# Hybrid encoder layer with expert-choice MoE on one core: attention preparation reordered, matmuls added during the first gather, two split rows instead of three on GpSimd, last result in halves

## The reference, cut to what matters

```python
proj = einsum('bsd,de->bse', rmsnorm(x), w_in)            # q, k, v, xr, gate
q, k = axial_rope(rmsnorm(q)), axial_rope(rmsnorm(k))
attn = softmax(q @ k.T * scale) @ v
lru  = (rglru_forward(conv(xr)) + rglru_backward(conv(xr))) * gelu(gate)
x    = x + concat(attn, lru) @ w_out
h    = rmsnorm(x)
affinity = softmax(h @ router_w)                          # (tokens, 16)
gate_vals, tok_idx = top_k(affinity.T, 64)                # per expert and group
xs  = take(h, tok_idx)
hid = silu(xs @ w_gate[e]) * (xs @ w_up[e])
ys  = (hid @ w_down[e]) * gate_vals
y   = x + zeros.at[tok_idx].add(ys)
```

## Time and profile before

| | us |
|---|---|
| median of 3 runs | 1058.98 (1057.98 to 1059.56) |
| profiled execution, time | 1058.12 |
| its span in the trace | 1056.2 |
| PE busy | 984.7 (93%) |
| DVE busy | 818.7 (78%) |
| ACT busy | 747.0 (71%) |
| POOL busy | 338.2 (32%) |
| share of PE in the chain that ended last | 82% |

### The profile page before, as it was taken

One profiled execution on the slowest core, in us unless ns is written; L12 is line 12 of the kernel. 1 busy time (PEld: TensorE's weight loads), 2 busy tenths in 40 slices (PEclk: granted clock), 3 DMA queues, 4 the chain that ended last, 5 costly groups with the idle time before them and its releaser, 6 DMA issues.

```text
span 1056.2 us, 15145 instructions
## 1 busy us (share of the span) xinstructions
PE 984.7 (93%) x5035; PEld 826.2 (78%) x5035; DVE 818.7 (78%) x1079; ACT 747.0 (71%) x1002; POOL 338.2 (32%) x175
## 2 busy tenths in 40 slices
PE   5999999977999999928999999999999999999994
PEld 4997998856777788827888888888888888888883
DVE  5749898787787224784989888988898889988983
ACT  6447888467797455545878877887788777877772
POOL 1000000132396111141056435643464346513320
PEclk9999999989999999968999999999999999999998
DMA  8110111000301633368999999999999999999842
GB/s 283 36 46 6 46 40 41 1 0 7 115 1 63 239 120 120 120 242 342 409 392 410 388 384 392 405 386 385 391 400 383 383 393 400 382 384 372 323 163 36
DMA packets 75265, 248.97 MB, mean 236 GB/s; under 512 B 9380, under 2 KB 16600, under 8 KB 75224
## 3 DMA queue, kind: packets, MB, share of 16 engines
q1 hardware_dynamic: 70616, 231.65, 57.1%
q0 software_dynamic: 4608, 16.78, 6.2%
HBM read 231.63 MB, written 16.78 MB: 235 GB/s over the span
## 4 chain that ended last, share of the span: by engine, by line
PE 82%; DVE 7%; ACT 5%; issue 3%; POOL 1%; DMA 1%; ACTq 0%; SPq 0%; POOLq 0%; DVEq 0%
PE bank L972 25%; PE bank L974 24%; PE bank L973 24%; PE bank L978 6%; DVE e_lo L1619 2%; ACT e_hi L899 2%; PE bank L1149 1%; PE bank L1107 1%; PE bank L1108 1%; PE bank L1007 1%; DMA x_nat<-in_x_prompt_dram 1%; ACT prob L843 1%; DMA xs<-h_rows,idx_all 0%; POOL prob L619 0%; DVE row_stat L1453 0%
## 5 line engine op out<-in xcount | busy, mean ns | idle before, releaser
L972 PE MATMUL bank<-e_hi,xsT_hi 128*128 128x512 f32 x512 | 202.4, 395 | 0.7 <-DVE xsT_lo L1624 0.6
L974 PE MATMUL bank<-e_hi,xsT_lo 128*128 128x512 f32 x512 | 200.5, 392 | 0.0
L973 PE MATMUL bank<-e_lo,xsT_hi 128*128 128x512 f32 x512 | 200.1, 391 | 0.0
L651 POOL COPY idx_now<-idx_all 128x1 uint32 (+1 forms) x16 | 157.1, 9818 | 27.2 <-DMA y_dram<-ys,idx_now 27.2
L899 ACT ACTIVATE e_hi<-raw_gate 128x1024 fp32r<-128x1024 f32 x128 | 134.7, 1062 | 35.3 <-PE bank L974 33.7
L1619 DVE TENSOR_TENSOR e_lo<-raw_down,e_hi 128x1024 fp32r<-128x1024 f32 x128 | 146.9, 1219 | 2.4 <-ACT e_hi L899 0.2
L1619 DVE TENSOR_TENSOR e_lo<-raw_gate,e_hi 128x1024 fp32r<-128x1024 f32 x125 | 144.7, 1219 | 4.8 <-ACT e_hi L899 4.7
L1619 DVE TENSOR_TENSOR e_lo<-raw_up,e_hi 128x1024 fp32r<-128x1024 f32 x128 | 146.7, 1219 | 1.4 <-ACT e_hi L899 1.3
L899 ACT ACTIVATE e_hi<-raw_up 128x1024 fp32r<-128x1024 f32 x128 | 126.5, 1057 | 1.3 <-PE bank L974 0.3
L899 ACT ACTIVATE e_hi<-raw_down 128x1024 fp32r<-128x1024 f32 x128 | 125.0, 1058 | 0.4 <-PE bank L974 0.3
L972 PEld LDWEIGHTS bank<-e_hi,xsT_hi 128*128 128x128 f32 x512 | 96.8, 189 | 21.4 <-DVE e_lo L1619 1.0
(11 more groups left out here) (241 smaller groups left out, 2193.9 us busy)
## 6 DMA issues: line engine op xcount, KB each, us to landing
raw_gate<-in_exp_w_gate_dram SPq DMA_DIRECT2D x64, 1024.0 KB, 10.8
raw_up<-in_exp_w_up_dram SPq DMA_DIRECT2D x64, 1024.0 KB, 8.2
raw_down<-in_exp_w_down_dram SPq DMA_DIRECT2D x64, 1024.0 KB, 7.0
w_raw<-in_w_in_dram SPq DMA_DIRECT2D x6, 1024.0 KB, 5.4
wo_raw<-in_w_out_dram SPq DMA_DIRECT2D x8, 512.0 KB, 4.2
y_dram<-x SPq DMA_DIRECT2D x8, 512.0 KB, 5.1
h_rows<-h SPq DMA_DIRECT2D x8, 512.0 KB, 2.6
x_nat<-in_x_prompt_dram SPq DMA_DIRECT2D x4, 512.0 KB, 7.5
```

The source lines that it names most:

```text
L651: pool.tensor_copy(idx_now[:, 2:3], idx_all[:, bass.ds(e, 1)] if not isinstance(e, int) else idx_all[:, e:e + 1]).then_inc(idx_copied, 1)
L972: pe.matmul(out, l_hi, r_hi, start=first, stop=False)
L973: pe.matmul(out, l_hi, r_lo, start=False, stop=False)
L974: return pe.matmul(out, l_lo, r_hi, start=False, stop=last)
```

## The change

Seven edits, in four places.

1. **Values.** `v_hi` and `v_lo` become one tensor for each group of tokens. The first group's split, and rotation and scaling of unit 9, move from slots 2 to 4 to `LRU_AT[27]`, which stands before the copy of job 27; the second group's split goes to slot 16. POOL zeroes each group's tensors apart.
2. **Places beside the slots.** The splits of blocks 4 to 7 move to slots 3/4, 8/9, 13/14 and 19/20. Transposes n from 12 on stand at 6, 8, 10, ... 28, and each copy in the slot of its transpose.
3. **Pairs 1 and 2.** Their first value matmuls are left out of their slot and done in the next, with that slot's own.
4. **During the first gather.** PE runs 16 matmuls 128x512 on `e_hi` row 0, whose results nothing reads, between the turned indices and the gathered tokens.
5. **Rows.** POOL writes the low parts of two rows of the first expert, DVE of the third too.
6. **Search.** In the last block, `find(1, 0)` stands behind the copy of `x2T`, and `find(1, 1)` behind `rstd2`.
7. **The end.** The last product runs rows 0 and 1 for both halves, then rows 2 to 7 for half 0, then for half 1. ACT scales each half by itself, and POOL scatters each half (128 rows of 512), with indices 2i and 2i+1 that DVE computes once behind `routed`.

```diff
-    v_hi = at("v_hi", R1 + 80 * K, [P, NB, VW], F32R)
-    v_lo = at("v_lo", R1 + 90 * K, [P, NB, VW], F32R)
+    v_hi = [at(f"v_hi{s}", R1 + o * K, [P, BPS, VW], F32R) for s, o in enumerate((80, 90))]
+    v_lo = [at(f"v_lo{s}", R1 + o * K, [P, BPS, VW], F32R) for s, o in enumerate((97, 85))]
...
-    SPLIT, POOL_ROWS = 6, 3
+    SPLIT, POOL_ROWS, WARM = 6, 2, 16
...
+    lru_at(27, ("v", 0), ("rotate", UNITS_QK - 1), ("norm", UNITS_QK - 1))
...
-    beside = {2: [('v', 0)], 3: [('rotate', 9)], 4: [('norm', 9)], 6: [('hi', 4)], 7: [('lo', 4)], 10: [('hi', 5)], 11: [('lo', 5)], 15: [('hi', 6)], 16: [('lo', 6)], 22: [('hi', 7)], 23: [('lo', 7)]}
+    beside = {3: [("hi", 4)], 4: [("lo", 4)], 8: [("hi", 5)], 9: [("lo", 5)], 13: [("hi", 6)], 14: [("lo", 6)],
+              16: [("v", 1)], 19: [("hi", 7)], 20: [("lo", 7)]}
     for n in range(2 * BPS, USES * NB):
-        at_slot = n - 2 * BPS + 1 if n < EARLY else 10 + (n - EARLY) * 5 // 3
+        at_slot = n - 2 * BPS + 1 if n < EARLY else 6 + (n - EARLY) * 2
         beside.setdefault(at_slot, []).append(("transpose", n))
-        beside.setdefault(at_slot + 1, []).append(("out", n))
+        beside.setdefault(at_slot, []).append(("out", n))
...
+    def late_pair(v):
+
+        return v % (2 * BPS) == 0 and 0 < v // (2 * BPS) < PAIRS_ONE_BANK
+
+    def pv_at(u):
+
+        v = u - V_LAG
+        if not 0 <= v < UNITS or late_pair(v):
+            return []
+        return [v - 1, v] if late_pair(v - 1) else [v]
...
-        for e in range(E - 4, E):
+        for e in range(E - 4, E - 1):
             scatter_step(e, 2 * (E - 4) + e - (E - 4) + 1)
+        y_halves = y.rearrange("t (h c) -> (t h) c", h=2)
+        pool.wait_ge(routed, 3)
+        for h in range(2):
+            pool.wait_ge(ys_done, E + 1 + h)
+            pool.sem_inc(scatter_ready, 1)
+            pool.indirect_dma_start(y_halves, bass.IndirectOffsetOnAxis(ap=idx_half[:, h:h + 1], axis=0),
+                                    ys[:, h * D // 2:(h + 1) * D // 2], None, compute_op=ALU.add).then_inc(scattered, 16)
+        pool.wait_ge(scattered, 16 * (E + 1))
...
-        act.wait_ge(row_used, 24 * E + 8)
-        results(E - 1)
+        act.wait_ge(ys_free, E)
+        for h in range(2):
+            act.wait_ge(row_used, 24 * E + 8 - SPLIT + h + 1)
+            act.activation(ys[:, h * D // 2:(h + 1) * D // 2], bank[:, 4 + h, :], ACT.Copy, scale=gate_all[:, E - 1:E]).then_inc(ys_done, 1)
...
+        pe.wait_ge(row_hi, 1)
+        for n in range(WARM):
+            pe.matmul(bank[:, n % 2, :], e_hi[:, 0, 0:P], e_hi[:, 0, 0:512], start=True, stop=True)
         pe.wait_ge(routed, 2)
         turn_tokens(16, 0)
...
-        rows(24 * E, 0, 4, hidT_hi, hidT_lo, {})
+        for j in range(8 - SPLIT):
+            pe.wait_ge(row_lo, 24 * E + j + 1)
+            for h in range(2):
+                ins = last_product(j, h)
+            ins.then_inc(row_used, 1)
+        for h in range(2):
+            for j in range(8 - SPLIT, 8):
+                if h == 0:
+                    pe.wait_ge(row_lo, 24 * E + j + 1)
+                ins = last_product(j, h)
+            ins.then_inc(row_used, 1)
...
-                find(1, 0)
                 dve.wait_ge(x2T_done, 2 * b + 1)
                 dve.wait_ge(logits_done, b - 1)
                 dve.tensor_copy(x2T[:, b % 2, 0:4, :], bank[:, 4, :].rearrange("p (k t) -> p k t", k=4)).then_inc(x2T_out_v, 1)
-                find(1, 1)
+                find(1, 0)
...
+        dve.wait_ge(routed, 1)
+        for h in range(2):
+            ins = dve.tensor_scalar(half_row[:, h:h + 1], idx_all[:, E - 1:E], 2.0, float(h), ALU.mult, ALU.add)
+        link(ins)
+        dve.tensor_copy(idx_half[:, :], half_row).then_inc(routed, 1)
```

63 lines of the change are left out of this document (41 added, 22 removed).

## The result

| | before | after |
|---|---|---|
| median (runs) | 1058.59 (4) | 1039.32 (1039.12 to 1039.55, 4) |
| span of the profiled execution | 1056.2 | 1037.0 |
| PE busy | 984.7 (93%) | 984.8 (95%) |

The ratio is 0.9817, 95% interval 0.980 to 0.9834: 19.3 us less. The forecast was 1038.2 (1033.5 to 1046.0). The spans differ by 19.2, and PE is busy as long as before: what went is waiting (span less busy time fell from 71.5 to 52.2). The 16 added matmuls do not show in PE's busy time, which fits a shorter time at half clock.

What follows compares the result with a forecast made beforehand. PE was taken as busy throughout the expert loop, so only its waits and half clock before or behind it count. Terms summed to 20.8 us off a median of 1058.98, giving 1038.2 us (range 1033.5 to 1046.0).

Steps and rivals of the forecast that it cites:

- attention's start: Values' split, rotation and scaling moved into DVE's 4.70 us hole: slot 9 starts 6.6 us sooner (4.5 to 7.5).
- bank 7: Slots 10 to 28: PE's four waits before transposes into bank 7 all go, 5.4 us (lower bound 2.7).
- pairs: Output bank at the change of pairs: two waits of 3.3 us shrink to 1.3, winning 2.0 us (0 to 3.3).
- half clock in attention: Half clock behind the 1.9 us wait at the change of pairs goes too: 1.6 us (0 to 1.6).
- two rows on GpSimd: Before the first expert: GpSimd ends its rows before DVE's merge, which takes 0.15; 1.6 us won (1.3 to 1.7).
- 16 matmuls: During the first gather: token transposes and first 36 expert matmuls run at full clock; 2.9 us won (0 to 3.9).
- the end: Last product, scaling and scatter in halves: PE held 0.7, scaling -0.5, scatter -0.9; sum -0.7 us (-1.8 to +0.8).
- the walk: Step-by-step timing of attention's slots: transposed probabilities may start at 215.1, first value product ends at 219.9, pair's product reached at 235.05.
- Rival 1: DVE sets attention's pace, with only 7% to spare: gain 14.0 us, time 1045.0; chance 0.21.
- Rival 4: Slower: attention's copies act as a lockstep, holding the next maximum and exponential while PE waits; 1068.6 us, chance 0.04.
- third rival: First gather held behind DVE's four rows, all behind it 3.8 us later: 1042.0, or 1044.9 without clock gain; chance 0.06.
- Rival 2: Clock does not rise in time: 16 matmuls all at half, 2.9 and 0.6 us lost, 1041.7; chance 0.07.

Runs made afterwards that it cites:

- m1_mix: Changed kernel with the copies of pairs 0 and 1 out of their bank one slot earlier on ACT and DVE; median 1039.40 us, ratio 0.9815.
- a2_places: Changed kernel with the late value matmuls of pairs 1 and 2 put back in their own slot; median 1041.55 us, ratio 0.9846.
- r3_rows: Changed kernel with three low rows on GpSimd again, not two; median 1040.66 us, ratio 0.9830.
- w0_no_warm: Changed kernel without the 16 matmuls ahead of the gathered tokens; median 1041.33 us, ratio 0.9838.
- f0_find: Changed kernel with the index search ahead of the x2T copy again; median 1039.46 us, ratio 0.9815.
- t0_tail: Changed kernel with the end of before: both halves in each row, one scaling, one scatter; median 1039.75 us, ratio 0.9815.
- g1_issue: Changed kernel with DVE's low rows made to wait for the first gather's issue, and 14 matmuls, not 16; median 1040.45 us, ratio 0.9827.

## Why the prediction held, and where it did not

| step | forecast | in the trace of after |
|---|---|---|
| attention's start | 6.6 | 5.6 |
| bank 7 | 5.4 | 5.4 |
| pairs | 2.0 | 1.0 |
| half clock in attention | 1.6 | 1.6 |
| slots 9 to 32, the rest | 0 | 1.1, of it 0.7 of two transposes now ahead of slot 9 |
| ahead of slot 0 | 0 | 0.5 |
| search, router | 0 | -1.1 |
| two rows on GpSimd | 1.6 | 1.6 |
| 16 matmuls | 2.9 | 2.9 |
| the end | 0.7 | 0.7 |
| sum | 20.8 | 19.2 (as rounded, 19.3) |

(The half clock is taken from the trace of before: the twelve matmuls and transposes from 263.56 last 3.98, and the same sequence from 257.77, at full clock, 2.37. The 0.4 that is left of the 1.1 was not traced.)

**Attention's start**: right in mechanism, and the walk's times came out within 0.2 us: transposed probabilities at 215.08 (215.1 in the walk), the first value product done by 220.07 (219.9). Part of that closeness is luck. Slot 0 began 0.48 sooner than in the trace of before, from which the walk set out, and this was lost again by 215.08: counted from slot 0, the product was done 0.65 later than in the walk. The rest of the 1.0 by which the term was too large is the transpose in slot 8 (0.36), which stands between that product and slot 9. The two transposes are not lost: they are missing from the stretch behind. The clock stayed at full speed, as assumed. The prediction says nothing of the half clock that the trace of before has here (219.6 to 226.4), though its term, taken from times of slot 9, holds what that cost; how much of it this is was not separated from the waits.

**Bank 7**: right: all four waits went, and DVE, with the reckoned 7% to spare, kept up. Rival 1 did not come. Rival 4 (lockstep of the copies) neither: the only wait for a copy in these slots is that of 0.93, at 216.67.

**Pairs**: the step that failed in size. "By the walk PE reaches it at 235.05 and the bank is copied out at 235.7": PE reached it at 235.7 (237.20 less 1.51), but the copy ended at 237.1. The walk took the copies as done almost as soon as the product ended; in the lists they stand behind an exponential on ACT and a maximum on DVE. Timelines of ACT, DVE and PE in the changed kernel:

```profile
235.16 0.69 ACT L874 ACTIVATE prob<-bank,row_stat 128x512 f32<-128x512 f32 x1 [0.65 <-DVE row_stat L1516]
...
235.83 0.59 ACT L859 ACTIVATE mixA_hi<-bank 128x512 fp32r<-128x512 f32 x1
```

```profile
235.70 0.68 DVE L1516 TENSOR_REDUCE row_stat<-bank 128x1 f32<-128x512 f32 x1
236.45 0.69 DVE L1522 TENSOR_TENSOR mixA_lo<-bank,mixA_hi 128x512 fp32r<-128x512 f32 x1
```

```profile
237.20 0.50 PE L1005 MATMUL bank<-probT_hi,v_hi 128*128 128x512 f32 x1 [1.51 <-DVE mixA_lo L1522]
```

m1_mix bears it out: with the copies moved ahead the waits are 0.9 in all, though the time up to slot 32 falls by 0.4 only. Yet the edit is worth more than either number, 3.6 us with the new places (a2_places), since without it the waits are 4.8 and the clock falls. The prediction had the same 3.6 as 2.0 and 1.6, but counted from the waits of before. Those were not the alternative: the new places alone lengthen the first pair's wait from 1.41 to 3.12.

**Two rows**: right, by r3_rows too. The doubt over the gather was settled the way of the trace, not of the third rival: the issue took 1.60, so 0.3 more than the 1.27 "kept". It waits for one DVE row, not for four. The Trainium skill ("SBUF — State Buffer", section "Who interferes with whom") says that a VectorE instruction with two SBUF inputs contends with GpSimd's reads, and (section "SBUF: two separate sides") that whichever starts first holds the pair for its whole instruction while the other blocks. By that the issue waits for the row in flight alone, and the thirteen traces agree (2.27 for the first issue, 4.32 for the second). The Trainium skill ("SBUF — State Buffer", section "Who interferes with whom") also infers that such a VectorE instruction does not hold up a GpSimd DMA, because making its descriptors takes the other interface. For these gathers the traces differ: the first issue took 1.27 to 2.14 with rows and 1.17 without. r3_rows shows the hold the other way round: the merge is held to the end of GpSimd's row.

**16 matmuls**: the number was right and the reason too, but two things in it are luck. The 0.3 that was taken off for holding the tokens' turning is 0.05 (w0_no_warm); what brought the tokens later, by 0.2, was the longer issue, which the sum had not. And the 0.5 of faster turning gave 0.9, of which 0.4 went into a longer wait for the tokens' low parts (0.97, before 0.56). Rival 2 did not come: the clock rose at 460.8, while the 16 ran. Nor is the worth fixed: it is 1.9 us in w0_no_warm. The trace of before, from which it was taken, had a late rise.

**Search**: 0 fits (f0_find, 0.2 off with 1.8 of noise). The -1.1 us beside it is the clock's, and the 0.5 us ahead of slot 0 as well: with the same instructions the clock rose at 20.4 in the trace of after and at 21.6 in that of before, in the first projection. Over the fourteen traces it rose between 19.2 and 21.9, and slot 0 came between 208.31 and 209.40, in nearly the same order. The Trainium skill ("TensorE: Matmul & The Clock Gate", section "What's actually happening") says that the number of slow matmuls at a start varies between runs of one kernel; these rows, of kernels with the same instructions up to there, agree.

**The end**: right term by term (0.9 of holding against 0.7, 0.4 against 0.5, 1.3 against 0.9), though no median shows it.

So the sum was 1.5 us too large (the median came out 1.1 above the forecast, as the median of before had come down by 0.4 with a fourth run): 1.0 of it is the pairs. The others cancel in part: attention's start 1.0 too large, the slots behind it 1.1 more than forecast, and -1.1 and +0.5 from where the clock fell and rose in two executions.

Of the signs that the prediction named, most came: the hole is filled, the merge takes 0.18, the first expert's matmuls run 0.23 apart at once, PE is held 0.9 in the last product, attention up to slot 32 is 14.7 us shorter, and PE waits for no load in the first experts (452 to 620). Two did not: PE has one wait over 1 us between slots 9 and 30 (1.51, the pairs), and the first gather is issued 0.5 us sooner counted from the last output product (20.6 against 21.1), not 1.6, since the router's last scores lost 1.1.

## What to carry to other kernels

Cost an edit against the schedule that will be there without it, not against the one before: the late pairs were worth 0 us in the old list and 3.6 in the new, and a sum of single terms shows neither. When a wait goes, walk the next one with every instruction that stands ahead of the releaser in its engine's list, copies included. And where an engine idles for a microsecond in several places, look for the clock there first: four runs of one kernel (t0_tail) were 4.1 us apart, in the order of their mean clock.

## What the runs showed of the hardware that was not expected

An indirect DMA's issue on GpSimd ended 2.27 us behind the start of DVE's rows of two SBUF inputs, whether it began 0.13, 0.68 or 1.00 us behind it; without such rows it took 1.17 and the next 0.95. Each time the end fits a wait for the DVE row in flight alone. A semaphore raised in GpSimd's program behind such an issue can be seen before the issue has run (g1_issue).

The granted clock fell to 0.50 in or behind waits of PE of 1.3 to 4.4 us, in g1_issue even behind two of 0.65 and 0.97; behind others as long (1.51 in the changed kernel, at 237.20) it did not. At the same place it fell in some traces and not in others: in seven of fourteen within the router's last scores (0.8 to 1.6 us lost) and in seven around the start of the last product (0.4 to 0.7 us lost in the kernels with halves, 2.9 in t0_tail). These are fourteen different kernels; that it varies within one is seen from the mean clock of its runs (0.983 to 0.989 in t0_tail). 14 matmuls ahead of the first expert left it to fall again, 16 or more did not in any of the traces that have them.
